# Rotations and query stacks at other steps of a woven attention, and four other orders of copies and read-outs, in a two-block fp32 kernel

## The reference, cut to what is computed

```python
# first block
h = h + memory_cross_attention(rms_norm(h, g), memn, w_q, w_k, w_v, w_xo)   # 4 heads of 256
# second block, for l in range(2)
z = rmsnorm(x, attn_norm[l]) @ w_in[l]          # qA kA vA fA, qB kB vB ..., qC kC vC gC, qD kD vD, gates
yA = forgetting_attention(qA, kA, vA, fA, bias)              # "fox", 8 heads, causal
yB = dsa_attention(rope(qB), rope(kB), vB, ...)              # "dsa", 8 heads, best 128 keys
r  = retention(rope(qC), rope(kC) / 8, vC)
yC = head_groupnorm(r, ret_norm) * silu(gC)
yD = sliding_window_gqa(rope(qD), rope(kD), vD, sinks)       # "swa"
x  = x + sum_n(sigmoid(gate_n) * (y_n @ w_branch_n)) @ w_out
x  = x + swiglu of a depthwise convolution of (rmsnorm(x) @ w_up), times w_down
```

## Time and profile before

| | us |
|---|---|
| median of 3 runs (3037.69 to 3039.84) | 3039.32 |
| the profiled execution, its own time | 3039.78 |
| its span | 3037.8 |
| TensorE busy | 2988.0 (98%) |
| VectorE busy | 1391.3 (46%) |
| ScalarE busy | 1289.9 (42%) |
| GpSimd busy | 1398.2 (46%) |
| granted TensorE clock, mean | 0.997 |

### The profile page before, as it was taken

One profiled execution on the slowest core, in us unless ns is written; L12 is line 12 of the kernel. 1 busy time (PEld: TensorE's weight loads), 2 busy tenths in 40 slices (PEclk: granted clock), 3 DMA queues, 4 the chain that ended last, 5 costly groups with the idle time before them and its releaser, 6 DMA issues.

```text
span 3037.8 us, 39928 instructions
## 1 busy us (share of the span) xinstructions
PE 2988.0 (98%) x15302; PEld 2438.1 (80%) x15302; DVE 1391.3 (46%) x2189; ACT 1289.9 (42%) x2219; POOL 1398.2 (46%) x1002
## 2 busy tenths in 40 slices
PE   8999999999999999999999999999999999999998
PEld 7778887788888777878888888878787788878887
DVE  7874351421113878562116433168776520264322
ACT  5443443433333446554234444244564533354432
POOL 5345574444444543234455454554332354544543
PEclk9999999999999999999999999999999999999999
DMA  5234242233333423223333333244231233333332
GB/s 158 83 112 144 87 132 91 77 97 97 99 97 85 142 69 89 53 67 87 97 93 99 94 97 99 83 109 138 68 91 42 64 98 97 97 94 97 97 97 71
DMA packets 214891, 287.61 MB, mean 95 GB/s; under 512 B 42682, under 2 KB 122610, under 8 KB 213042
## 3 DMA queue, kind: packets, MB, share of 16 engines
q1 hardware_dynamic: 212210, 279.88, 31.5%
q0 software_dynamic: 880, 2.99, 0.3%
q10 hardware_dynamic: 1616, 2.23, 0.2%
HBM read 269.80 MB, written 4.72 MB: 90 GB/s over the span
## 4 chain that ended last, share of the span: by engine, by line
PE 89%; DVE 6%; ACT 2%; POOL 1%; issue 1%; DMA 0%; ACTq 0%; SPq 0%; DVEq 0%
PE half L732 80%; PE half L1169 1%; PE half L1155 1%; PE half L1226 1%; POOL wL L2917 1%; PE half L1138 1%; PE half L1133 1%; DVE arena L2082 1%; DVE arena L2681 1%; DVE arena L2715 1%; PE half L987 0%; PE half L1004 0%; DVE rms L2073 0%; PE half L1212 0%; DVE arena L2706 0%
## 5 line engine op out<-in xcount | busy, mean ns | idle before, releaser
L2917 POOL TENSOR_TENSOR wL<-slot,wH 128x512 fp32r<-128x512 f32 (+1 forms) x976 | 1366.5, 1407 | 1610.1 <-ACT wH L1336 1609.0
L1336 ACT ACTIVATE wH<-slot 128x512 fp32r<-128x512 f32 (+1 forms) x976 | 603.4, 625 | 1229.3 <-PE half L732 1223.7
L732 PE MATMUL half<-nH,wH 128*128 128x512 f32 x2336 | 922.6, 395 | 8.1 <-POOL wL L2917 3.1
L732 PE MATMUL half<-nH,wL 128*128 128x512 f32 x2336 | 910.2, 390 | 0.0
L732 PE MATMUL half<-nL,wH 128*128 128x512 f32 x2336 | 909.7, 389 | 0.0
L732 PE MATMUL half<-arena_split,wH 128*128 128x512 f32 (+1 forms) x2432 | 735.8, 385 | 1.7 <-issue 0.8
L732 PEld LDWEIGHTS half<-nH,wH 128*128 128x128 f32 x2336 | 438.5, 188 | 119.7 <-issue 20.2
L732 PEld LDWEIGHTS half<-arena_split,wH 128*128 128x128 f32 x2432 | 451.2, 188 | 94.6 <-issue 3.4
L732 PEld LDWEIGHTS half<-nH,wL 128*128 128x128 f32 x2336 | 438.5, 188 | 92.6
L732 PEld LDWEIGHTS half<-nL,wH 128*128 128x128 f32 x2336 | 438.8, 188 | 89.2 <-issue 1.4
L732 PE MATMUL half<-arena_split,wL 128*128 128x512 f32 (+1 forms) x1216 | 466.4, 384 | 0.0
(11 more groups left out here) (351 smaller groups left out, 2656.5 us busy)
## 6 DMA issues: line engine op xcount, KB each, us to landing
slot<-in_w_in SPq DMA_DIRECT2D x344, 256.0 KB, 2.7
slot<-in_w_up SPq DMA_DIRECT2D x440, 128.0 KB, 2.2
slot<-in_w_down SPq DMA_DIRECT2D x132, 256.0 KB, 2.6
slot<-in_w_branch SPq DMA_DIRECT2D x64, 256.0 KB, 2.6
slot<-in_w_out SPq DMA_DIRECT2D x48, 256.0 KB, 2.8
slot<-in_w_gate SPq DMA_DIRECT2D x88, 128.0 KB, 2.1
arena<-arena SPq DMA_DIRECT2D x40, 256.0 KB, 4.4
slot<-in_w_proj_b SPq DMA_DIRECT2D x16, 256.0 KB, 2.9
```

The costliest lines, as they stand in the source:

```text
L732: mm = pe.matmul(dst, lhsT, rhs, start=(k == 0 and m == 0), stop=(k == last and m == 2))
L1336: act.activation(wH[:, p, 0:cols], slot[:, s, 0:cols], ACT.Copy).then_inc(weights_high, 1)
L2917: pool.tensor_tensor(wL[:, p, 0:cols], slot[:, s, 0:cols], plainly(wH[:, p, 0:cols]), ALU.subtract)\
```

## The change

It makes no instruction more or less in number, apart from one read-out that is cut off from its group and one product unit that is issued in two halves. It changes where they stand:

1. The last unit of `awq1` is multiplied for banks 0 and 1 first, then for 2 and 3; ScalarE copies banks 0 and 1 after the first half. The count of `bank_done` shifts by one for its users at the end.
2. Bank 0 of the gate `bgt2a` is read ahead of the copy of the turned probabilities in its iteration.
3. Units 4 and 5 of `bup2` are rounded behind ScalarE's Silu of group 0 and behind its `round_ff`, and 6 and 7 in group 1; before, 4 to 7 stood together in group 1 behind `conv_last`.
4. The gating of the retained output (L2807) stands at iteration 1 of the sliding attention ahead of the reciprocal and the scaling, not behind them.
5. In the woven attention the rotation of qB goes from iterations 0, 1, 3 to -1, 0, 1; that of qC from 6 (ahead of the reciprocal), 7, 9 to 4, 8, 12 (behind the scaling); that of kC from 13, 15, 17 to 14, 16, 18. `STACK_AT` goes from 9, 11, 17, 21 to 5, 9, 18, 22, so the remainders on VectorE from 10, 12, 18, 22 to 6, 10, 19, 23.

```diff
-STACK_AT = (9, 11, 17, 21)
+STACK_AT = (5, 9, 18, 22)
...
# TensorE, queries_of
-                    unit(ps[1], "awq1", k, stream)
+                    if k < KD - 1:
+                        unit(ps[1], "awq1", k, stream)
+                    else:
+                        unit(ps[1], "awq1", k, stream, part=[0, 1]).then_inc(S["bank_done"], 1)
+                        unit(ps[1], "awq1", k, stream, part=[2, 3]).then_inc(weights_used, 1)
...
# ScalarE
-            def evac_by_bank(to, h, func=ACT.Copy, **kw):
-
-                for j in range(4):
+            def evac_by_bank(to, h, func=ACT.Copy, part=range(4), **kw):
+
+                for j in part:
...
+            act.wait_ge(S["bank_done"], 1)
+            act.activation(xq[:, 4:6, :], banks(1)[:, 0:2, :], ACT.Copy).then_inc(S["xq_read"], 1)
             done(act, "awq1")
-            act.activation(xq[:, 4:6, :], banks(1)[:, 0:2, :], ACT.Copy).then_inc(S["xq_read"], 1)
...
                     s = weave.first + it
+                    if ("bgt2a", KD - 1) in weave.at(it):
+                        done(act, "bgt2a", l)
+                        act.wait_ge(S["yc_split"], l + 1)
+                        evac_by_bank(gate_b[2], jobs.half["bgt2a"], part=[0])
                     if weave.has(it):
                         turned(s, False)
...
-                    elif n == 2:
-                        act.wait_ge(S["yc_split"], l + 1)
                     h = jobs.half[name]
                     if n < 3:
-                        evac_by_bank(gate_b[n], h)
+                        evac_by_bank(gate_b[n], h, part=range(1, 4) if n == 2 else range(4))
...
-                    if 0 < g < NG - 1:
+                    if g == 1:
+                        round_units("bup2", l, 0, [6, 7], 512)
+                    elif 0 < g < NG - 1:
                         others(f"bup{g + 1}", l)
...
                     act.activation(conv[:, p, 0:2, :], conv[:, p, 0:2, :], ACT.Silu).then_inc(S["silu"], 1)
+                    if g == 0:
+                        round_units("bup2", l, 0, [4], 512)
                     act.wait_ge(S["ff_ready"], l * NG + g + 1)
                     round_ff(conv[:, p, 0:2, :], g)
+                    if g == 0:
+                        round_units("bup2", l, 0, [5], 512)
...
# VectorE
                     if amid:
-                        rope(*amid)
+                        amid()
...
-                pieces = {0: ("bqB", qB, 1, [0]), 1: ("bqB", qB, 1, [1]), 3: ("bqB", qB, 1, [2]),
-                          7: ("bqC", qC, 2, [1]), 9: ("bqC", qC, 2, [2]),
-                          13: ("bkC", kC, 3, [0]), 15: ("bkC", kC, 3, [1]), 17: ("bkC", kC, 3, [2]),
+                pieces = {-1: ("bqB", qB, 1, [0]), 0: ("bqB", qB, 1, [1]), 1: ("bqB", qB, 1, [2]),
+                          4: ("bqC", qC, 2, [0]), 8: ("bqC", qC, 2, [1]), 12: ("bqC", qC, 2, [2]),
+                          14: ("bkC", kC, 3, [0]), 16: ("bkC", kC, 3, [1]), 18: ("bkC", kC, 3, [2]),
...
-                    woven(WEAVE_A, it, ("bqC", qC, 2, [0]) if it == 6 else None)
+                    woven(WEAVE_A, it)
...
-                    woven(WEAVE_S, it)
+                    woven(WEAVE_S, it, retained_gated if it == TURN_C else None)
...
-                dve.wait_ge(S["bank_done"], k - 3)
+                dve.wait_ge(S["bank_done"], 1 + k - 3)
```

More of the change, by code:

```diff
@@ L2792, in _, with retained_gated @@
                 dve.tensor_tensor(grouped, grouped, wide(mean, HD), ALU.subtract).then_inc(S["group_centred"], 1)
+                def retained_gated():
+                    dve.wait_ge(S["gc_ready"], l + 1)
+                    dve.wait_ge(S["y_turned"], l + 1)
+                    h = jobs.half["btC"]
+                    for c in range(NB):
+                        ins = dve.scalar_tensor_tensor(out=gC[:, c, :], in0=ps[h][:, c * T:c * T + T],
+                                                       scalar=vec[:, W_RET + c:W_RET + c + 1], in1=gC[:, c, :],
+                                                       op0=ALU.mult, op1=ALU.mult)
+                        if c < 3:
+                            ins.then_inc(S["bank_read"], 1)
+                    ins.then_inc(S["yc_ready"], 1)
+                    dve.wait_ge(S["yc_ready"], l + 1)
+                    dve.sem_inc(drained[h], 1)
                 for it in WEAVE_S.its:
-                    woven(WEAVE_S, it)
+                    woven(WEAVE_S, it, retained_gated if it == TURN_C else None)
                     if it == -AHEAD:
@@ L2801, in _ @@
                         dve.tensor_tensor(grouped, grouped, wide(mean, HD), ALU.mult).then_inc(S["group_normed"], 1)
[L2802 to L2814, removed]
                     if it == TURN_C + 2:
```

## The result

The changed kernel took 3056.07 us (median of 6 runs, 3053.66 to 3057.41), the kernel before beside it 3038.51 (6 runs): a ratio of 1.0057, interval 1.0046 to 1.0068. It is slower by 0.6%. The profiled execution took 3054.77 us with a span of 3052.8, so 15.0 us more than the span before (3037.8).

The account below looks back on a forecast made before the run. TensorE, busy for 2988.0 of 3037.8 us, was taken as the bound, so only its pauses were summed: 3039.78 - 6.0 (edits 1 to 4) + 21.8 (edit 5) = 3055.6, for the median 3055.1 us; range 3043 to 3064.

Parts of the forecast that it names:

- the old 1.88 stays: Woven attention: iteration 10 keeps a remainder, so the existing 1.88 us pause before the scores of 12 remains.
- the sum: Edit 5's new pauses in the weave, added place by place: 10.9 us in each layer, 21.8 us in both.
- the early time: Woven attention: start of the scores, less 0.06 us for the signal, less the last maximum's end; 0.5 us at iterations 4 and 8.
- meeting with a subtraction: Woven attention: GpSimd's subtraction, due during a long rotation, goes ahead of VectorE's next SBUF operation; 1.3 us more.
- VectorE first: Rival, woven attention: VectorE's next operation goes ahead of the waiting subtraction; edit 5 costs 13.8 us, total 3047.1 us; chance 0.24.
- Late transfers: Rival: kC's swapped rows land late or loads behind them hold ScalarE; 2 to 4 us more per layer, some 3062 us; chance 0.10.
- The other side: Rival, weave: VectorE's queue decides, not the scaling's end; old pauses go, moved rotations sit in free time; 3027.1 us; chance 0.10.
- Nothing on balance: Rival: the weave's edits do nothing on balance, half of the pauses falling away; costs 5 to 8, 3038 to 3042 us; chance 0.06.

Follow-up runs that it names:

- short subtraction: The changed kernel with GpSimd's subtraction cut to 8 of 512 columns for the units of qC, kC, vC, qD and gC; 3028.04 us, ratio 0.996.
- edits 1 to 4 alone: The changed kernel with edit 5 taken back (stacks and rotations as before); 3032.17 us, ratio 0.9982 against the kernel before.

## Why the prediction was right, and where its working wasn't

The forecast was 3055.0 us in a range of 3043 to 3064, slower with 0.84. The time was 3056.07. The direction, the mechanism and the place of nearly all pauses held. The pauses were priced 4.8 us too high, a term of 5.1 us was missing, and the two cancel.

**Edits 1 to 4**: forecast 6.0 us. Measured 5.8 us in pauses and 5.3 us by the medians (span 5.0). `bup2` gave 1.31 of the forecast 1.4, the others their whole wait.

**Edit 5, place by place** (forecast; measured in layer 0 and 1 by the timeline):

| pause before the scores of | forecast | layer 0 | layer 1 |
|---|---|---|---|
| 6 (rotation at 4) | 3.1 | 2.81 | 2.81 |
| 8 (remainder at 6) | 1.9 | 0.92 | 1.50 |
| 10 (rotation at 8) | 3.1 | 2.81 | 2.81 |
| 12 (the old 1.88 stays) | 1.88 | 1.52 | 1.52 |
| 14 (rotation at 12) | 0.9 | 0.66 | 0.66 |
| 16 (rotation at 14) | 0.8 | 0.58 | 0.58 |
| 18 (rotation at 16) | 1.0 | 0.81 | 0.81 |
| 20 (rotation at 18) | 0.1 | 0 | 0 |

The new idle time is 8.2 and 8.8 us, 17.0 where the sum said 21.8. At the two dearest places the early time of 0.5 us was right. In the kernel with the rotation of kC alone nothing stands at iteration 4, and its timeline (VectorE, then TensorE) has

```profile
1134.35 2.43 DVE L2694 SCALAR_TENSOR_TENSOR arena<-consts,ftm,arena 128x512 f32<-128x512 f32 x2
1137.42 0.69 DVE L2719 CUSTOM_DVE_ANT_0 arena<-half,arena 128x512 f32<-128x512 f32 x1
1138.65 0.70 PE L1142 MATMUL half<-arena 64*128 64x256 f32 x4
```

so the maxima are over 0.54 us before the scores, 0.48 less the signal. The 0.47 us at iteration 9 are of the same kind, with this bias ahead of them in the kernel before:

```profile
1155.50 2.43 DVE L2681 SCALAR_TENSOR_TENSOR arena<-consts,ftm,arena 128x512 f32<-128x512 f32 x2
```

Both bias pairs last 2.43 us in place of 1.40, so one meeting with a subtraction is in these 0.5 us already. A rotation put in brings a second one, and only that has to be added: it was priced at 1.3 us and took 1.0. 2.28 + 1.0 - 0.5 = 2.8, against 2.28 + 1.3 - 0.5 = 3.1. The short subtraction gives the same sum from the other end: without any meeting the maxima are 1.5 us early, and then both must be paid, 2.28 + 1.07 + 0.97 - 1.5 = 2.8. The other differences are of a kind: the old pause before 12 came down to 1.52 us, and those before 14, 16 and 18 were 0.2 us under their price. At the pause before 8, the largest miss (0.92 and 1.50 for 1.9), the size was right by itself, as the run with the stacks alone shows, but the sum treated neighbouring places as independent.

**The missing term** is the clock. The prediction said that TensorE's busy time stays the same; it rose by 4.4 us, and in the weave three drops cost 5.1 us. With the 17.0 us this makes 22.1 in the weave, where 21.8 was forecast; had the clock stayed, the forecast would have been 5 us too high. That the total is right to 1 us is luck. It was there to be read: the windows of the trace of before show three drops behind pauses, and the longest new pauses should have been given a chance of one each.

**The rivals.** VectorE first: no, the bias behind the rotations lasted 2.38 and not 1.4 us, and the short subtraction shows what that is worth. Late transfers: VectorE doesn't sit idle before the rotation of kC; no pause is of that kind. The other side (the queue's load decides): no, the pauses before 4 and 12 stay (1.15 and 1.52), and the rotations are not free. Nothing on balance: it happens at one place, in one kernel (the pause before 12 with qC at 4, 8, 9), by the timing of a subtraction.

**Left open**: whether GpSimd's operation meets the bias differs between the layers of one kernel by tenths of a microsecond (0.92 and 1.50 above; with edits 1 to 4 alone, which touch nothing there, 0.86 us stood new before the scores of 6 in layer 0, and in layer 1 the old pause before 12 was 0.77 in place of 1.87), and no row before the change tells on which side it falls. How many drops a typical execution has, and not the profiled one, wasn't measured. That the stacks alone cost 8.4 us by the medians and 5.3 by the spans comes from the executions that were profiled: that of edits 1 to 4 alone was the slowest of its ten, 2.6 us over their median, for a reason that isn't known.

## What to carry to other kernels

Price an operation moved into a loop between two engines by what it delays next, and count the meetings with the third engine that it adds: in this kernel a rotation of 2.28 us delays the maxima by 3.3, since it pushes the bias behind it into a second subtraction of GpSimd. Slack read from a trace goes with the meetings that this trace already has (0.5 us with one of them); slack without any is had by making the suspected engine's work short (1.5 us), and then every meeting has to be paid. The two must not be mixed. Where a moved operation leaves TensorE a new pause, look at the granted clock behind the pauses of that size that the trace already has, and add what it shows there.

## What the runs showed of the hardware that I had not expected

Behind pauses of TensorE the granted clock fell to some 0.5, mostly 1.7 us of lost time each: behind 22 of 24 pauses of 2.7 to 2.9 us, 22 of 32 of 1.7 to 1.9 us, and none of 30 of 1.1 to 1.5 us. Equal pauses at the same place of two kernels (1.88 and 1.86 us) gave a clock of 1.00 and 0.59. Two subtractions of GpSimd, 1.58 and 1.37 us, stretched one pair of bias operations from 1.15 to 3.22 us, and the second started 0.19 us after the first had ended.
